# Weight blocks placed between the steps of a chunked linear attention, in a two-block transformer layer on one core

## The chip, the core and the metric

The kernel runs on one NeuronCore of one Trainium2 chip. The metric is the device time of one execution in microseconds (us), lower is better. The engines named are TensorE (PE, with its weight loads PEld), VectorE (DVE), ScalarE (ACT), GpSimd (POOL) and SyncE (SP, which issues the weight transfers).

## The reference, cut to what matters

The program computes two blocks on a sequence of 256 tokens of width 2048. The change touches only the token mixer of the second block:

```
def token_mixer(h, w_in, ...):
    z = h @ w_in                                  # 2048 columns in, 12304 out
    z_sg, q, k, v, og, g_lr, m_a, m_b = split(z)  # q, k: 1024 columns; v, og, m_a, m_b: 2048
    ...                                           # y_a from z_sg
    log_a = max(log_sigmoid(g_lr @ w_gate2 + b) / 16, -1)
    o = gla_chunked(q, k, v, log_a)               # 4 heads, 4 chunks of 64 tokens
    y_b = rmsnorm(o, gla_norm_g) * silu(og)
    merged = sigmoid(m_a) * (y_a @ w_proj_a) + sigmoid(m_b) * (y_b @ w_proj_b)
    return merged @ w_out

def gla_chunked(q, k, v, log_a):                  # for each head, over chunks of 64 tokens
    bcum = cumsum(log_a); b_last = bcum[last]
    q_in = q * dk**-0.5 * exp(bcum); k_in = k * exp(-bcum); k_st = k * exp(b_last - bcum)
    attn = causal(q_in @ k_in.T); o_intra = attn @ v
    step: o_inter = q_in @ state; state = state * exp(b_last) + k_st.T @ v
    return o_intra + o_inter
```

The output gate `og` is not needed by `gla_chunked`, and `m_b` is needed by neither the attention nor its normalisation.

## The kernel before, in words

Activations are kept transposed in SBUF as two fp32r tensors, a high part and the low rest (`HT`/`r_a` for the mixer's input, `YT`/`r_b` for the branch that is projected). A weight matrix is read in **blocks** of 512 output columns, and a block in **chunks** of 256 input rows (512 KB each). For each chunk SP issues a transfer into a ring of 5 slots (`raw_ring`), ACT rounds it to a high part (`act_hi`, L573, into one of 3 slots of `w_hi`), DVE subtracts that to leave the low part (`dve_lo`, L579, written over the raw slot), and PE multiplies (`pe_block_part`, L602): 2 tiles of 128 tokens x 2 row tiles x 3 products (high by high, high by low, low by high), 12 matmuls of 512 columns, into PSUM bank 0 for the first tile and bank 1 for the second. PE's last matmul of a chunk raises `pair_used`, for which the cast three chunks on and the transfer five chunks on wait. After the 8 chunks of a block ACT moves the two banks to SBUF and raises `acc_free`, for which the first matmuls of the next block wait.

All engines run programs written out by hand, in order, with semaphores. Nothing reorders them, so that an instruction whose semaphore is late holds up all that follow on its engine.

In the mixer the phase `qkvo` has 12 blocks: 0 and 1 are q, 2 and 3 are k, 4 to 7 are v, and 8 to 11 are `og`. All 12 are multiplied first, `og` with Silu at its evacuation. Then comes the linear attention, `gla_body(i)` for 4 heads. PE's steps in a head are: cumulative sums of the decay in banks 4 and 5 (L1050, L1051); transposes of the block sum (L1056, bank 6); transposes of `QIN` and `KIN` (L1063, banks 7 and 0); scores (L1069, bank 1); `delta(0)` (L1075, banks 2 and 3); scores by v (L1088, L1089), `inter(1)` (L1082) and `delta(1)`; `inter(2)` and `delta(2)`; `inter(3)`. Between two of these steps there is a hand-over: ACT copies, takes exponentials or evacuates (L1521 to L1540), DVE scales, masks and updates the state (L2116 to L2137), and PE waits. These matmuls are plain fp32, which the trace shows as two records each. After the heads, ACT and DVE normalise `o` (L1241, L2152), DVE multiplies by the gate (L2155), and PE transposes the product into `YT` (phase `yb`, L782, with ACT at L1215 and DVE at L1687 behind it). Then the phase `mb` starts: 4 blocks of 16 chunks, 8 of `m_b` from `HT`, evacuated through Sigmoid (L1452), and 8 of `w_proj_b` from `YT`, merged by DVE (L2088, L2089).

Of the kernel before, what the change touches and what calls it, by code (L numbers as in the profile page):

```python
# [19 lines left out]
P = 128  # L20
# [74 lines left out]
def build(nc, A, out, xs):  # L95
    ds = bass.ds
    ctx = ExitStack()
    with ctx:
# [296 lines left out]
        gl_qk, gl_dec, gl_decs, gl_tr, gl_qt = sem("gl_qk"), sem("gl_dec"), sem("gl_decs"), sem("gl_tr"), sem("gl_qt")  # L395
        gl_att, gl_dl, gl_st, gl_o, gl_of = (sem("gl_att"), sem("gl_delta"), sem("gl_state"),
# [375 lines left out]
        def _(pe):  # L772
# [268 lines left out]
            for i in range(12):  # L1041
                qkvo_body(i)
            pe.wait_ge(tr_free, TRN["gl"][0] + 4)
            pe.wait_ge(gl_a, 1)

            def gla_body(i):
                pe.wait_ge(gl_of, 2 * i + 1)
                for t in range(2):
                    la = LOGA[:, t, ds(i * GK, GK)]
                    nc.tensor.matmul(PS[:, 4 + t, 0:GK], CN[:, C_TRI:C_TRI + P], la, start=True, stop=True)  # L1050
                    nc.tensor.matmul(PS[:, 4 + t, GK:2 * GK], CN[:, C_BLK:C_BLK + P], la, start=True,  # L1051
                                     stop=True).then_inc(gl_cum, 1)
                pe.wait_ge(gl_bcs, 2 * i + 2)
# [25 lines left out]
                def inter(n):  # L1079
# [120 lines left out]
        def _(act):  # L1200
# [278 lines left out]
            si = evac_to("qkvo", ph, 7, 2, lambda t, b: ZQ[:, t, ds(b * NB, NB)], ACT.Silu)  # L1479
# [33 lines left out]
            for i in range(2, 9):  # L1513
                q_body(i, cp)
            for i in range(9, 12):
                q_body(i, si)
            si(11)

            def gla_body(i):
                act.wait_ge(gl_cum, 2 * i + 1)  # L1520
# [6 lines left out]
                nc.scalar.activation(E2, BCS[:, :, 0:GK], ACT.Exp, scale=-1.0).then_inc(gl_exp, 1)  # L1527
                act.wait_ge(gl_df, i + 1)
                nc.scalar.activation(E3, E3, ACT.Exp).then_inc(gl_exp, 1)
                act.wait_ge(gl_dec, i + 1)  # L1530
# [3 lines left out]
                for k, (dst, b) in enumerate(((QT, 7), (KT2, 0))):  # L1534
                    act.wait_ge(gl_tr, 2 * i + k + 1)
                    nc.scalar.copy(dst, PS[:, b, :].rearrange("p (d n) -> p d n", d=2)).then_inc(gl_qt, 1)
                for t in range(2):
                    act.wait_ge(gl_o, 2 * i + t + 1)
# [136 lines left out]
        def _(dve):  # L1675
# [433 lines left out]
            for i in range(3, 12):  # L2109
                for j in range(8):  # L2110
                    dve_lo(dve, PH["qkvo"], i, j)

            def gla_body(i):
                qs, ks = ZQ[:, :, ds(i * GK, GK)], ZQ[:, :, ds(GH * GK + i * GK, GK)]
                dve.wait_ge(gl_bcs, 2 * i + 2)
                TT(E3, BCS[:, :, GK:2 * GK], BCS[:, :, 0:GK], ALU.subtract).then_inc(gl_df, 1)  # L2116
                dve.wait_ge(gl_exp, 3 * i + 1)
                V.scalar_tensor_tensor(QIN, qs, GK ** -0.5, E1, ALU.mult, ALU.mult).then_inc(gl_qk, 1)
                dve.wait_ge(gl_exp, 3 * i + 2)
                TT(KIN, ks, E2, ALU.mult).then_inc(gl_qk, 1)  # L2120
                dve.wait_ge(gl_exp, 3 * i + 3)
                TT(KST, ks, E3, ALU.mult).then_inc(gl_qk, 1)
                for n in range(3):
                    dve.wait_ge(gl_dl, 3 * i + n + 1)
# [19 lines left out]
            V.tensor_scalar(SSO, SSO, 1.0 / GV, EPS, ALU.mult, ALU.add).then_inc(ms_ready, 1)  # L2144
            dve.wait_ge(rt_ready, m + 1)
# [11 lines left out]
            merge_loop("mb", 16, True)  # L2157
# [150 lines left out]
```

## Time and profile before

| | |
|---|---|
| median of 3 runs | 4530.18 us (4527.86 to 4532.74) |
| the profiled execution | 4539.61 us |
| its span in the profile | 4537.8 us |
| PE busy | 4114.8 us, 91% |
| DVE busy | 1732.0 us, 38% |
| ACT busy | 1631.0 us, 36% |
| granted TensorE clock, mean | 0.892 of 2.4 GHz |

The median is what the changed kernel is compared with, while durations come from the one profiled execution, which took 9.4 us (0.2%) more. "Busy" of PE counts modelled ends of matmuls: a PE that is busy may be running at half its clock, so the granted clock has to be read beside it. Times of rows are from the start of the span.

### The profile page before, as it was taken

What the parts mean: (1) busy time and instruction counts of PE and PEld (TensorE: products, weight loads), DVE (VectorE), ACT (ScalarE), POOL (GpSimd) and SP (SyncE); (2) the same over time, 40 slices, a digit from 0 to 9 for tenths busy, and PEclk for the clock granted to TensorE, in tenths of its full rate; (3) what the DMA queues carried; (4) which work ended last, traced back from release to release, by engine and by line L of the source; (5) the groups of instructions that cost most, each with busy time, mean ns of one, the idle gap of its engine ahead of it and who ended that gap; (6) DMA issues with size and microseconds to landing.
All of it is one profiled execution on the core that took longest, in us unless ns stands there. A gap on an engine that the chain in (4) does not pass through costs nothing.

```text
span 4537.8 us, 46263 instructions
## 1 busy us (share of the span) xinstructions
PE 4114.8 (91%) x19088; PEld 3106.5 (68%) x19088; DVE 1732.0 (38%) x2643; ACT 1631.0 (36%) x2550; POOL 69.1 (2%) x120
## 2 busy tenths in 40 slices
PE   5899979998899999989988989999789987999998
PEld 1466656676566667865666767787267767999886
DVE  0322233322223233333224545443255445666544
ACT  1222123334312123333344343444234455555433
POOL 3000000000001000000000000000000000000000
PEclk8899985569899999995598999999799998999999
DMA  9444420001245443320024555565045444666564
GB/s 316 141 147 141 148 77 1 1 18 35 75 148 167 158 139 95 115 82 1 6 65 121 191 149 163 171 188 169 0 155 171 158 138 127 195 193 193 181 199 153
DMA packets 350594, 577.49 MB, mean 127 GB/s; under 512 B 25252, under 2 KB 130868, under 8 KB 348208
## 3 DMA queue, kind: packets, MB, share of 16 engines
q1 hardware_dynamic: 344000, 549.39, 38.7%
q0 software_dynamic: 6384, 25.14, 1.8%
q8 instruction: 151, 2.47, 0.2%
q14 instruction: 59, 0.48, 0.0%
HBM read 570.26 MB, written 4.19 MB: 127 GB/s over the span
## 4 chain that ended last, share of the span: by engine, by line
PE 52%; DVE 5%; ACT 4%; issue 1%; DMA 0%; ACTq 0%; DVEq 0%
PE ps L602 32%; PE ps L1176 11%; PE ps L695 2%; PE ps L916 1%; DVE w_lo L579 1%; PE ps L686 1%; PE ps L885 1%; ACT w_hi L573 1%; PE ps L1075 1%; PE ps L1082 1%; PE ps L864 1%; ACT f_arena L1222 0%; PE ps L622 0%; DVE r_a L1689 0%; DVE r_b L1687 0%
## 5 line engine op out<-in xcount | busy, mean ns | idle before, releaser
L579 DVE TENSOR_TENSOR w_lo<-raw_ring,w_hi 128x1024 fp32r<-128x1024 f32 (+1 forms) x827 | 1003.1, 1223 | 1539.2 <-ACT w_hi L573 1530.9
L573 ACT CAST w_hi<-raw_ring 128x1024 fp32r<-128x1024 f32 (+1 forms) x827 | 858.6, 1049 | 1585.4 <-PE ps L602 751.0
L602 PE MATMUL ps<-w_hi,r_a 128*128 128x512 f32 x3552 | 1285.5, 403 | 74.8 <-DVE w_lo L579 49.4
L602 PE MATMUL ps<-w_lo,r_a 128*128 128x512 f32 x2624 | 1040.0, 396 | 0.0
L602 PEld LDWEIGHTS ps<-w_hi,r_a 128*128 128x128 f32 x3552 | 678.7, 191 | 346.0 <-issue 129.1
L602 PE MATMUL ps<-w_hi,r_b 128*128 128x512 f32 x2272 | 862.2, 399 | 9.3 <-DVE w_lo L579 4.2
L602 PEld LDWEIGHTS ps<-w_lo,r_a 128*128 128x128 f32 x2624 | 502.2, 191 | 105.3
L602 PEld LDWEIGHTS ps<-w_hi,r_b 128*128 128x128 f32 x2272 | 435.1, 192 | 114.3 <-DVE w_lo L579 11.4
L1176 PE MATMUL ps<-r_a,w_hi 128*128 128x256 f32 x2816 | 480.6, 277 | 3.0 <-DVE w_lo L579 3.0
L1176 PEld LDWEIGHTS ps<-r_a,w_hi 128*128 128x128 f32 x2816 | 425.5, 188 | 3.1 <-issue 3.1
L1176 PE MATMUL ps<-r_a,w_lo 128*128 128x256 f32 x1408 | 389.4, 277 | 0.0
L1176 PEld LDWEIGHTS ps<-r_a,w_lo 128*128 128x128 f32 x1408 | 265.2, 188 | 0.0
L695 PE MATMUL ps<-f_arena 128*128 128x64 f32 (+1 forms) x1072 | 226.8, 379 | 15.1 <-DVE f_arena L743 14.4
L637 PE MATMUL ps<-raw_ring,silu_c_t 128*2 128x512 f32 x768 | 201.0, 657 | 39.2 <-DMA raw_ring<-in_w_ada_dram 32.4
L695 PEld LDWEIGHTS ps<-f_arena 128*128 128x128 f32 x1072 | 220.8, 300 | 22.8 <-issue 22.0
L602 PE MATMUL ps<-w_hi,act_t 128*128 128x512 f32 x704 | 221.4, 395 | 5.8 <-DVE w_lo L579 5.4
L705 ACT ACTIVATE f_arena<-ps,neg_max 128x512 f32<-128x512 f32 (+1 forms) x164 | 99.9, 609 | 349.9 <-DVE neg_max L731 180.2
L686 PEld LDWEIGHTS ps<-consts,f_arena 128*128 128x128 f32 x536 | 84.8, 199 | 170.9 <-issue 106.7
L728 DVE TENSOR_REDUCE neg_max<-ps 128x1 f32<-128x512 f32 (+1 forms) x164 | 97.4, 594 | 187.4 <-PE ps L941 139.8
L916 PE MATMUL ps<-raw_ring,f_arena 128*128 128x192 f32 (+1 forms) x816 | 157.2, 355 | 8.0 <-ACT f_arena L1398 5.7
L686 PE MATMUL ps<-consts,f_arena 128*128 128x128 f32 x536 | 141.6, 402 | 20.7 <-ACT f_arena L714 14.5
L782 PE MATMUL ps<-consts,f_arena 128*128 128x128 f32 x508 | 91.3, 332 | 75.2 <-ACT f_arena L1236 35.6
(289 smaller groups left out, 3057.2 us busy)
## 6 DMA issues: line engine op xcount, KB each, us to landing
raw_ring<-in_w_in_dram SPq DMA_DIRECT2D x386, 512.0 KB, 3.7
raw_ring<-in_w_ada_dram SPq DMA_DIRECT2D x192, 512.0 KB, 3.9
raw_ring<-in_ffn_w_up_dram SPq DMA_DIRECT2D x176, 512.0 KB, 3.6
raw_ring<-in_w_out_dram SPq DMA_DIRECT2D x96, 512.0 KB, 3.7
raw_ring<-in_ffn_w_down_dram SPq DMA_DIRECT2D x88, 512.0 KB, 3.7
raw_ring<-in_w_proj_b_dram SPq DMA_DIRECT2D x32, 512.0 KB, 3.6
raw_ring<-in_w_proj_a_dram SPq DMA_DIRECT2D x16, 512.0 KB, 3.5
raw_ring<-in_w_qb_dram SPq DMA_DIRECT2D x24, 288.0 KB, 3.0
```

The lines of the kernel that those rows point to most:

```text
L573: nc.scalar.copy(WH[:, ph.s_slot(i, j), 0:n], RAW[:, ph.raw_slot(i, j), 0:n]).then_inc(hi_ready, 1)
L579: nc.vector.tensor_tensor(WL[:, ph.raw_slot(i, j), 0:n], RAW[:, ph.raw_slot(i, j), 0:n], WH[:, ph.s_slot(i, j), 0:n].bitcast(F32), ALU.sub ...
L602: mm = nc.tensor.matmul(PS[:, ti, 0:cols], X(x, k, t), W[w][:, kk * cols:(kk + 1) * cols], start=(k == 0 and q == 0), stop=(c == len(js) - ...
L637: mm = nc.tensor.matmul(PS[g:g + 2, 7, :], SCT[:, k, :], RAW[:, ph.raw_slot(i, j), kk * NB:(kk + 1) * NB], start=(k < ADAG), stop=(k >= KT ...
L686: tr = nc.tensor.transpose(PS[:, 6, q * P:q * P + P], PB[:, u % 2, q * P:q * P + P], ident)
L695: mm = nc.tensor.matmul(PS[:, 7, 0:vdim], PT[:, u % 2, q * P:q * P + P], V(u, kt), start=(q == 0), stop=(q == len(kts) - 1))
L705: ins = nc.scalar.activation(PB[:, k % 2, 0:w], PS[:, 4 + k % 2, 0:w], ACT.Exp, bias=NM[:, k % 2:k % 2 + 1], accum_out=SUM[:, k % 2:k % 2 ...
L728: mx = nc.vector.tensor_reduce(NM[:, k % 2:k % 2 + 1], PS[:, 4 + k % 2, 0:w], AX_X, ALU.max, negate=True)
L782: return [lambda b, t=t: nc.tensor.transpose(PS[:, b, t * P:t * P + P], src(t), ident) for t in range(T)]
L864: yield nc.tensor.matmul(PS[:, 4 + k % 2, 0:kr.stop - kr.start], QTA[r, t * P:t * P + P], KTA[r, kr], start=True, stop=True)
L916: mm = nc.tensor.matmul(PS[:, t, o:o + cols], X[:, k, t * P:t * P + P], RAW[:, ph.raw_slot(i, j), kk * cols:(kk + 1) * cols], start=(k == ...
L1176: mm = nc.tensor.matmul(PS[:, 4 * b + f, 0:256], W[w][:, kk * 256 + f % 2 * P:kk * 256 + f % 2 * P + P], HT[:, x, k, :], start=(k == 0 and ...
```

## The change

Three things are done, all inside the mixer's second branch:

1. `qkvo` blocks 8 to 11 (`og`) are taken out of the row of 12 and multiplied inside the heads of the linear attention. Each head now holds one block, with one chunk ahead of each of the eight places at which PE waits for ACT or DVE. ACT and DVE have their `act_hi` and `dve_lo` for these chunks written between their own steps, two chunks ahead of PE. The blocks are evacuated plain, in the head.
2. Banks 0 and 1 now hold those blocks, so the transposed `KIN` goes to bank 6 and the scores to bank 7. PE's transposes of `KIN` get a new wait on `gl_decs`, since ACT has to have read bank 6.
3. The first 8 chunks of `mb` (block 0 of `m_b`) are multiplied straight after the last head, while ACT and DVE normalise. ACT now takes the Silu of `og` there in two instructions of 128 x 2048, and DVE multiplies by the gate in two halves (new semaphore `gl_og`). PE no longer waits for all 16 evacuated transposes before the first `w_proj_b` chunk, but for as many as each chunk reads.

The core of the diff, PE, ACT and DVE in this order. `si` is the evacuation of a block with Silu, `cp` the plain one. Left out are, on PE, four more `next(og)` ahead of the waits for `gl_qk` 3i+3, `gl_att`, `gl_st` 3i+2 and `gl_st` 3i+3, and on ACT and DVE eight `next` each in `gla_body`, and on ACT `cp(8 + i)` ahead of the wait for `inter(3)`:

```
-            for i in range(12):
+            for i in range(8):
                 qkvo_body(i)
+            def og_chunks():
+                for b in range(8, 12):
+                    for c in range(8):
+                        pe_block_part(pe, PH["qkvo"], b, S8, c, 2, NB, hT, range(2), AC["qkvo"][b])
+                        yield
+            og = og_chunks()
             def gla_body(i):
+                next(og)
                 pe.wait_ge(gl_of, 2 * i + 1)
...
+                next(og)
                 pe.wait_ge(gl_bcs, 2 * i + 2)
...
+                next(og)
                 pe.wait_ge(gl_qk, 3 * i + 2)
-                for X, b in ((QIN, 7), (KIN, 0)):
+                for X, b in ((QIN, 7), (KIN, 6)):
+                    if b == 6:
+                        pe.wait_ge(gl_decs, i + 1)
...
+                next(og)
                 pe.wait_ge(gl_qt, 2 * i + 2)
...
-                        mm = nc.tensor.matmul(PS[:, 1, t * P:t * P + P], KT2[:, d, t * P:t * P + P],
+                        mm = nc.tensor.matmul(PS[:, 7, t * P:t * P + P], KT2[:, d, t * P:t * P + P],
...
             for i in range(GH):
                 gla_body(i)
+            pe_block(pe, PH["mb"], 0, S8, 2, NB, hT, range(2), AC["mb"][0])
             pe.wait_ge(gl_of, 2 * GH + 2)
             for k in range(KT):
                 group(TRN["yb"][0] + k, tr_tiles(lambda t: ZQ[:, t, OGO + k * P:OGO + k * P + P], 2))
-            pe.wait_ge(tr_free, TRN["yb"][0] + KT)
...
+                for c in range(8):
+                    if i == 0:
+                        pe.wait_ge(tr_free, TRN["yb"][0] + 2 * c + 2)
+                    pe_block_part(pe, PH["mb"], i, list(range(8, 16)), c, 2, NB, yT, range(2), acc_at("mb", i, 2, 1))
```
```
-            for i in range(9, 12):
-                q_body(i, si)
-            si(11)
+            act_hi(act, ph, 8, 0)
+            cp(7)
+            act_hi(act, ph, 8, 1)
+            def og_his():
+                seq = [(ph, b, j) for b in range(8, 12) for j in range(8)] + [(PH["mb"], 0, 0), (PH["mb"], 0, 1)]
+                for p, b, j in seq[2:]:
+                    act_hi(act, p, b, j)
+                    yield
...
             nc.scalar.copy(JG[0][:, 0:8], SSO.rearrange("p t h -> p (t h)")).then_inc(ss_ready, 1)
+            act_hi(act, PH["mb"], 0, 2)
             root("gla", SSO, RIO)
+            act_hi(act, PH["mb"], 0, 3)
+            ogs = ZQ[:, :, OGO:OGO + D]
+            nc.scalar.activation(ogs[:, 0], ogs[:, 0], ACT.Silu)
+            act_hi(act, PH["mb"], 0, 4)
+            nc.scalar.activation(ogs[:, 1], ogs[:, 1], ACT.Silu).then_inc(gl_og, 1)
+            for j in range(5, 9):
+                act_hi(act, PH["mb"], 0, j)
+            sig_evac("mb", 0)
             to_hi("yb", KT, lambda k: YT[:, 0, k, :], 256)
-            sig_loop("mb", 16)
+            sig_loop("mb", 16, 1)
```
```
             V.tensor_scalar(SSO, SSO, 1.0 / GV, EPS, ALU.mult, ALU.add).then_inc(ms_ready, 1)
+            dve_lo(dve, PH["mb"], 0, 2)
...
                     ins = V.scalar_tensor_tensor(o, o, RIO[:, t, h:h + 1], GNB, ALU.mult, ALU.mult)
+                    if h % 2:
+                        dve_lo(dve, PH["mb"], 0, 3 + 2 * t + h // 2)
             L(ins)
-            TT(og, og, ZQ[:, :, VO:VO + D], ALU.mult).then_inc(gl_of, 1)
+            dve.wait_ge(gl_og, 1)
+            TT(og[:, 0], og[:, 0], ZQ[:, 0, VO:VO + D], ALU.mult)
+            dve_lo(dve, PH["mb"], 0, 7)
+            TT(og[:, 1], og[:, 1], ZQ[:, 1, VO:VO + D], ALU.mult).then_inc(gl_of, 1)
+            dve_lo(dve, PH["mb"], 0, 8)
```

The order on PE, in the first half of a head, before (L1051 is the second of the cumulative sums, L1056 and L1063 transposes, L1069 the scores, L1075 `delta`):

```order
L1051 MATMUL ps<-gla_arena,consts 128x256
L1056 MATMUL ps<-consts,gla_arena 128x128 x4
L1063 MATMUL ps<-consts,f_arena 128x128 x8
L1069 MATMUL ps<-gla_arena 128x128 x4
L1075 MATMUL ps<-gla_arena,f_arena 128x512 x2
```

The same place now (the lines have moved: L1066 was L1056, L1076 was L1063, L1083 was L1069, and L603, which was L602, is the matmul of a weight block):

```order
L1066 MATMUL ps<-consts,gla_arena 128x128 x4
L603 MATMUL ps<-w_hi,r_a 128x512
...
L603 MATMUL ps<-w_hi,r_a 128x512
L1076 MATMUL ps<-consts,f_arena 128x128 x8
L603 MATMUL ps<-w_hi,r_a 128x512
...
L603 MATMUL ps<-w_hi,r_a 128x512
L1083 MATMUL ps<-gla_arena 128x128 x4
```

Each group of L603 rows holds 12 matmuls, one chunk. Nothing is taken out of the head itself.

The order on ACT in a head now (L574 is the cast `act_hi`, L1547 the copy of v, L1550 the copies of the sums, L1552, L1553 and L1556 the exponentials, L1559 the decay, L1565 the copies of the transposed q and k, L1574 and L1575 the evacuation of `o`, L1279 the evacuation of the weight block):

```order
L1550 COPY gla_arena<-ps 128x512 x2
L1552 ACTIVATE f_arena<-gla_arena 128x512
L1553 ACTIVATE f_arena<-gla_arena 128x512
L574 CAST w_hi<-raw_ring 128x1024
L1556 ACTIVATE f_arena<-f_arena 128x512
L574 CAST w_hi<-raw_ring 128x1024
L1559 ACTIVATE decay<-ps 128x8
L574 CAST w_hi<-raw_ring 128x1024
L1565 COPY gla_arena<-ps 128x512 x2
L574 CAST w_hi<-raw_ring 128x1024 x2
L1574 ACTIVATE f_arena,gla_sums<-ps 128x512
```

Before, none of the four L574 rows stood there. The casts now stand ahead of steps that PE and DVE wait for.

The order on DVE in the normalisation after the heads, before (L2146 is the reciprocal of the root, L2152 the scaling, L2155 the product with the gate):

```order
L2146 RECIPROCAL gla_rinv<-gla_rinv 128x8
L2152 SCALAR_TENSOR_TENSOR f_arena<-f_arena,gla_rinv,gla_arena 128x512 x8
L2155 TENSOR_TENSOR f_arena<-f_arena 128x2x2048
L1687 TENSOR_TENSOR r_b<-ps,r_b 128x256 x16
```

And now (L580 is `dve_lo`, L2208, L2214, and L2220 with L2222 are the three steps):

```order
L2208 RECIPROCAL gla_rinv<-gla_rinv 128x8
L2214 SCALAR_TENSOR_TENSOR f_arena<-f_arena,gla_rinv,gla_arena 128x512 x2
L580 TENSOR_TENSOR w_lo<-raw_ring,w_hi 128x1024
...
L2214 SCALAR_TENSOR_TENSOR f_arena<-f_arena,gla_rinv,gla_arena 128x512 x2
L580 TENSOR_TENSOR w_lo<-raw_ring,w_hi 128x1024
L2220 TENSOR_TENSOR f_arena<-f_arena 128x2048
L580 TENSOR_TENSOR w_lo<-raw_ring,w_hi 128x1024
L2222 TENSOR_TENSOR f_arena<-f_arena 128x2048
```

Five L580 rows now stand between the reciprocal and the last product, and one more ahead of the reciprocal.

## Rows read from the trace of the kernel before

**Rows 1.** The page: busy time of the engines.
```profile
PE 4114.8 (91%) x19088; PEld 3106.5 (68%) x19088; DVE 1732.0 (38%) x2643; ACT 1631.0 (36%) x2550; POOL 69.1 (2%) x120
```

**Rows 2.** Stretches: length, busy time of the engines, clock, DMA share, GB/s.
```profile
3104.80:3127.20 22.40, 22.27 (x97) 17.95 (x97) 9.69 (x9) 9.39 (x10) 0.00 (x0) 1.00 0.65 188
3161.00:3298.00 137.00, 99.98 (x226) 41.40 (x224) 28.05 (x44) 29.72 (x59) 0.00 (x0) 0.75 0.02 6
```

**Rows 3.** PE's groups in 3161 to 3298: busy, mean ns, idle before.
```profile
L1082 PE MATMUL ps<-gla_arena 128*64 128x512 f32 x48 | 29.2, 740 | 12.0 <-DVE gla_arena L2133 12.0
...
L1088 PE MATMUL ps<-gla_arena 128*128 128x512 f32 x8 | 8.3, 1141 | 6.9 <-DVE gla_arena L2137 6.9
...
L1063 PE MATMUL ps<-consts,f_arena 128*128 128x128 f32 x32 | 7.1, 394 | 6.6 <-DVE f_arena L2120 6.6
...
L1050 PE MATMUL ps<-gla_arena,consts 128*128 128x256 f32 x16 | 5.1, 398 | 3.8 <-ACT f_arena L1540 3.8
```

**Rows 4.** PE in the first head, in order of time: start, duration.
```profile
3172.18 3.78 PE L1075 MATMUL ps<-gla_arena,f_arena 64*128 64x512 f32 x4
...
3187.45 1.93 PE L1082 MATMUL ps<-gla_arena 128*64 128x512 f32 x4 [1.50 <-DVE gla_arena L2133]
...
3189.31 1.98 PE L1075 MATMUL ps<-gla_arena,f_arena 64*128 64x512 f32 x4
...
3192.79 3.40 PE L1082 MATMUL ps<-gla_arena 128*64 128x512 f32 x4 [1.50 <-DVE gla_arena L2133]
```

**Rows 5.** Stretches of 4 us around the end of the first head; columns as rows 2.
```profile
3186.00:3190.00 4.00, 2.55 (x6) 0.92 (x7) 1.39 (x2) 0.00 (x0) 0.00 (x0) 1.00 0.00 0
3190.00:3194.00 4.00, 2.50 (x6) 0.64 (x5) 1.41 (x2) 0.00 (x0) 0.00 (x0) 0.89 0.00 0
...
3198.00:3202.00 4.00, 2.09 (x11) 1.35 (x9) 1.34 (x3) 3.36 (x6) 0.00 (x0) 1.00 0.00 0
```

**Rows 6.** ACT and DVE in order of time: a chunk's cast and subtraction, then a head's hand-overs.
```profile
3144.85 1.05 ACT L573 CAST w_hi<-raw_ring 128x1024 fp32r<-128x1024 f32 x1 [2.12 <-PE ps L602]
3145.93 1.23 DVE L579 TENSOR_TENSOR w_lo<-raw_ring,w_hi 128x1024 fp32r<-128x1024 f32 x1 [1.94 <-ACT w_hi L573]
...
3162.19 1.04 ACT L1521 COPY gla_arena<-f_arena 128x1024 f32<-128x1024 f32 x1 [0.32 <-PE ps L1051]
3163.14 1.07 ACT L1524 COPY gla_arena<-ps 128x512 f32<-128x512 f32 x2
3164.23 1.28 ACT L1526 ACT_TABLE_LOAD   x1
...
3165.52 0.63 ACT L1526 ACTIVATE f_arena<-gla_arena 128x512 f32<-128x512 f32 x1
...
3166.18 0.69 DVE L2118 SCALAR_TENSOR_TENSOR f_arena<-f_arena 128x512 f32<-128x512 f32 x1 [1.25 <-ACT f_arena L1526]
```

**Rows 7.** The chain of waits after the last head: start, length, what.
```profile
3299.47 1.28 ACT L1241
3300.76 0.22 ACT gla_rinv L1241
...
3301.24 5.40 DVE f_arena L2152 x8
...
3306.66 4.43 DVE f_arena L2155
...
3318.66 1.84 issue
3320.50 24.90 PE ps L602 x96
...
3368.02 12.18 PE ps L602 x52
```

**Rows 8.** ACT in order of time: an activation of 128 x 2048.
```profile
2918.74 1.92 ACT L1493 ACTIVATE f_arena<-gla_arena 128x2048 f32<-128x2048 f32 x1
```

**Rows 9.** A stretch of later transposes (L782); columns as rows 2.
```profile
3516.00:3518.00 2.00, 2.00 (x12) 1.00 (x10) 2.00 (x7) 2.00 (x6) 0.00 (x0) 1.00 0.00 0
```

More of the change, by code:

```diff
@@ L1084, in inter @@
                     return mm
+                next(og)
                 pe.wait_ge(gl_qk, 3 * i + 3)
                 delta(0)
+                next(og)
                 pe.wait_ge(gl_att, i + 1)
@@ L1092, in gla_body @@
                 delta(1)
+                next(og)
                 pe.wait_ge(gl_st, 3 * i + 2)
@@ L1095, in gla_body @@
                 delta(2)
+                next(og)
                 pe.wait_ge(gl_st, 3 * i + 3)
@@ L1512, in _ @@
                            (3, log_abs, ()), (4, log_exp, ()), (5, log_ln, ())])
-            for i in range(2, 9):
+            for i in range(2, 8):
                 q_body(i, cp)
-            for i in range(9, 12):
-                q_body(i, si)
-            si(11)
+            act_hi(act, ph, 8, 0)
[6 more added lines that the diff above has]
+                    yield
+            og = og_his()
             def gla_body(i):
+                next(og)
                 act.wait_ge(gl_cum, 2 * i + 1)
@@ L1527, in gla_body @@
                 nc.scalar.activation(E2, BCS[:, :, 0:GK], ACT.Exp, scale=-1.0).then_inc(gl_exp, 1)
+                next(og)
                 act.wait_ge(gl_df, i + 1)
                 nc.scalar.activation(E3, E3, ACT.Exp).then_inc(gl_exp, 1)
+                next(og)
                 act.wait_ge(gl_dec, i + 1)
@@ L1533, in gla_body @@
                                      ACT.Exp).then_inc(gl_decs, 1)
-                for k, (dst, b) in enumerate(((QT, 7), (KT2, 0))):
+                next(og)
+                for k, (dst, b) in enumerate(((QT, 7), (KT2, 6))):
                     act.wait_ge(gl_tr, 2 * i + k + 1)
                     nc.scalar.copy(dst, PS[:, b, :].rearrange("p (d n) -> p d n", d=2)).then_inc(gl_qt, 1)
+                next(og)
+                next(og)
                 for t in range(2):
+                    if t:
+                        next(og)
+                        next(og)
+                        cp(8 + i)
                     act.wait_ge(gl_o, 2 * i + t + 1)
@@ L2108, in _, with og_los @@
                         V.tensor_scalar(G[:, 0:2048], LM, 1.0 / 16.0, -1.0, ALU.mult, ALU.max).then_inc(gl_a, 1)
-            for i in range(3, 12):
+            for i in range(3, 8):
                 for j in range(8):
                     dve_lo(dve, PH["qkvo"], i, j)
+            dve_lo(dve, PH["qkvo"], 8, 0)
+            dve_lo(dve, PH["qkvo"], 8, 1)
+            def og_los():
+                seq = [(PH["qkvo"], b, j) for b in range(8, 12) for j in range(8)] + [(PH["mb"], 0, 0), (PH["mb"], 0, 1)]
+                for p, b, j in seq[2:]:
+                    dve_lo(dve, p, b, j)
+                    yield
+            og = og_los()
             def gla_body(i):
+                next(og)
                 qs, ks = ZQ[:, :, ds(i * GK, GK)], ZQ[:, :, ds(GH * GK + i * GK, GK)]
@@ L2116, in gla_body @@
                 TT(E3, BCS[:, :, GK:2 * GK], BCS[:, :, 0:GK], ALU.subtract).then_inc(gl_df, 1)
+                next(og)
                 dve.wait_ge(gl_exp, 3 * i + 1)
@@ L2120, in gla_body @@
                 TT(KIN, ks, E2, ALU.mult).then_inc(gl_qk, 1)
+                next(og)
                 dve.wait_ge(gl_exp, 3 * i + 3)
                 TT(KST, ks, E3, ALU.mult).then_inc(gl_qk, 1)
+                next(og)
+                next(og)
                 for n in range(3):
+                    if n:
+                        next(og)
                     dve.wait_ge(gl_dl, 3 * i + n + 1)
@@ L2137, in gla_body @@
                         V.copy_predicated(ATT, bc(CN[:, C_TRI:C_TRI + P].bitcast(I32), 2),
-                                          PS[:, 1, 0:256].rearrange("p (t n) -> p t n", t=2)).then_inc(gl_att, 1)
+                                          PS[:, 7, 0:256].rearrange("p (t n) -> p t n", t=2)).then_inc(gl_att, 1)
+                next(og)
             for i in range(GH):
```

10 lines of the change are left out of this document (4 added, 6 removed).

## The prediction, made before the changed kernel was run

> **What bounds the kernel now.** I read the page's busy times first. PE is busy 91% of the span and no other engine over 38% [rows 1], so that time is won where PE idles or runs at half clock. Then two stretches side by side [rows 2]: a block of the `qkvo` phase, where PE is busy 22.27 of 22.40 us at a granted clock of 1.00, and the four heads, 137.00 us with PE busy 99.98 at 0.75. That stretch begins when block 11 ends (3161) and holds no weight block at all; DVE and ACT are busy 28 and 30 us in it, and the DMA share is 0.02. So PE idles 37.0 us there, and of the 100 in which it works a part is at 1.2 GHz. PE's groups name most of it [rows 3]: 12.0 + 6.9 + 6.6 + 3.8 = 29.3, each time for the ACT or DVE step just before; by difference 7.7 are left for L1056 and L1069. Third, the chain of waits after the last head [rows 7]: the last `inter(3)` ends at 3298.0, the first `mb` matmul starts at 3320.5, that block takes 24.9, and its `w_proj_b` part ends at 3368.0. That is 70.0 us for 16 chunks, against 44 at the rate of rows 2.
>
> **Part 1, the heads.** Before: four `og` blocks at 22.4 [rows 2] are 89.6, and with the heads' 137.0 it is 226.6 us.
>
> After, PE has the same matmuls and, if nothing is late, no gaps. A block is 96 matmuls; inside a block they start 0.2288 us apart (22.27 / 97 is 0.2296 with its boundary), so a chunk of 12 takes 2.75 and a block 22.0. The boundary gap of about 0.4 goes, since the evacuation now has other PE work beside it. A head's own matmuls are taken at full clock. L1075 is the yardstick: the same four records take 3.78 us early in the head and 1.98 later, L1082's four 1.93 [rows 4]. One group starts 1.87 after the other. There are seven such groups (three `delta`, three `inter`, one for scores by v); without the modelled end of the last record, which overlaps what follows, 1.75 each, 12.3. L1050 has 16 records of 256 columns, and L1051 as many: half of the columns of those above, so about 0.22 a record, and with 8 in a head 1.7. L1063 is 7.1 us in four heads for 32 records, mostly at half clock, so at full clock about 1.1 a head with the part that is already fast; L1069 has as many records of the same shape, and L1056 half as many: 1.1 and 0.5 [rows 3]. The sum is 16.7, and I take 17.
>
> So PE needs 39.0 a head. Now whether hand-overs are hidden. Each has a chunk of 2.75 ahead of it. Durations on ACT and DVE [rows 6]: a cast 1.05, a subtraction 1.23, a copy of v 1.04, the two copies of sums 1.07, an exponential about 0.6, a product about 0.65. I follow the tightest one, q and k, from the end of the first cumulative sum (time 0). ACT: v to 1.1, sums to 2.1, two exponentials to 3.3, cast to 4.35 (its wait is for the chunk before the sums, long used). DVE: subtraction to 5.6, QIN to 6.3, KIN to 6.95. PE: second sum to 0.9, chunk to 3.6, L1056 to 4.1, chunk to 6.8. PE is ready 0.15 before KIN. All others have slack: the copies that L1069 waits for end at 9.1 where PE comes at 10.7; state and mask after `delta(0)` take 1.7 of the next chunk's 2.75, and the later state updates 1.4; the last evacuation of `o` takes 1.25 of the next head's first chunk. The new wait on `gl_decs` ends at 6.2, before PE comes. The casts for chunks two ahead are each released by a chunk that PE has already done, because the order is the same on all three engines. What is queued behind each of them is the hand-over, and that is in the sum above. I add 0.2 a head, and once 1.3 in the first head for the table load of the exponential, which sits in this tightest chain [rows 6]. ACT needs about 17 us a head and DVE as much (a quarter of rows 2's 29.7 and 28.1, plus 8 casts or subtractions), under half of PE's 39.
>
> After: 4 x (39.0 + 0.2) + 1.3 = 158.1. Gain: 226.6 - 158.1 = 68.5 us, of which 37 is idle time, about 30 the clock, less 1.5 for waits, and the rest boundaries and tails.
>
> **The clock.** This is the term that has to be argued. In 3186 to 3194 PE was busy 5 of 8 us, with half-filled arrays only (64 rows or 64 columns), and the clock was 1.00 for the first four and fell within the next (0.89). `inter(3)` then ran slow, 3.40 us of L1082 without a gap [rows 4], and from 3198, just after it, the clock was 1.00 again [rows 5]. So PE's continuous work in the heads' own shapes brings the clock up, and after the change over half of the time is dense blocks. I take 1.00 for the whole stage.
> The Trainium skill, in TensorE: Matmul & The Clock Gate, section "A second HAM failure mode: psum-queue depth-cycling", says that a kernel which cycles through PSUM banks can idle in such small pieces between groups that the clock swings all the same, and the changed stage visits seven banks. By it the present mean of 0.75 would stay, which is priced below as a rival; the dense stretch in rows 2, which alternates two banks, does not swing.
>
> **Part 2, normalisation and first `mb` block.** Time 0 is the end of `inter(3)` (3298.0 before). PE: eight chunks from 0 to 22.0 if their low parts are there. ACT: evacuation to 1.25, sums copied 1.5, cast 2 to 2.5, table and root to 4.0, cast 3 to 5.05, table 1.28 and Silu 1.92 [rows 7, 8] to 8.25, cast 4 to 9.3, second Silu to 11.2, cast 5 to 12.25, then casts at PE's pace. DVE: subtraction 2 to 3.75, reciprocal 4.2, scaling 1.35 a pair (5.40 / 4) with subtractions 3, 4, 5, 6 between, which end at 6.8, 10.55, 13.5 and 16.1. PE wants them at 8.2, 11.0, 13.7 and 16.5: just in time. Half of the gate product is 2.2 (4.43 / 2): first to 18.3, subtraction 7 to 19.55 (PE wants it at 19.2: 0.35 late), second to 21.8, so `gl_of` is there when PE ends the block at 22.3. The whole chain of 13.1 us from 3298.0 to the transposes has grown by the subtractions, but lies beside PE's block. Then 16 transposes at DVE's pace: Sigmoid evacuates to 23.4, DVE starts at 23.85 and takes 0.42 for each, PE may issue the last four earlier and goes on at about 29.2. Before, 1.84 lay between the last split and the first matmul; that goes. Eight chunks are 22.0, plus 0.7 because chunk 9's cast stands behind all evacuations: 51.9. The clock: it was 1.00 at later transposes at this pace [rows 9]; I allow 1.1 us. So 53.0 in place of 70.0, a gain of 17.
> Bounds: 19 if nothing of this is late, and 10 if the chain, six subtractions and two Silus come one after another (13.1 + 7.4 + 3.8, which is 2.3 past the block) and the clock falls as in rows 7 (24.9 for 22.0).
> The Trainium skill, in ScalarE: Activation LUTs, section "What ACT_TABLE_LOAD costs", has every change of table drain for 1.38 us more behind the 1.28 of the load. Two such changes stand ahead of cast 4; by the rule subtraction 4 ends at 13.3, PE loses 2.3 us, and the sum is 4446. The trace has the root start 0.01 us after the load [rows 7], so I leave it at nothing.
>
> **Sum.** 68.5 + 17 = 85.5 from the profiled 4539.6 gives 4454.1; the median of the runs is 9.4 below the profiled execution, so from 4530.2 it gives 4444.7, and I say 4444. After this stage nothing is moved. The extra transfers are none; they only move into a stretch whose DMA share is 0.02.
>
> **Rivals.**
> A. The clock keeps swinging. For: mean 0.75 in the same stage today, and the half-filled arrays remain. Against: rows 5. If only the heads' own matmuls stay as slow as now, they take their 100 us, not 68: 4444 + 32 = 4476. If all 156 us run at a mean of 0.75, it is 208: 4496.
> B. Hand-overs are late. For: the tightest one has no slack, and both queues are strict. Each of eight places late by half a cast (0.5) costs 4 x 8 x 0.5 = 16, by a whole one 34: 4460 to 4478. Against: seven of eight have over 1 us in hand by the rows.
> C. The change doesn't shorten the stage, because each chunk is only put in front of a hand-over and nothing lies beside it: then the four blocks cost 88 in the heads as outside, and only part 2 is gained: 4513. Against: the casts are two chunks ahead in all three programs.
> D. Slower: PE falls to 1.2 GHz for the interleaved stage, dense chunks too, since small gaps at every hand-over keep it there. Of 156 us of PE work the share g run at half clock adds 156 g; above g = 0.55 it eats the 85.5. At g = 1 it is 4600. Against: the clock rose within the heads even with the gaps [rows 5].
>
> **Chances.** Forecast (4434 to 4456) 0.72; B 0.13; A 0.09; C 0.03; D 0.03. The low end is the forecast with 17 a head at 15.5, 6 less, and 19 in part 2, with 2 for the runs: 4434. The high end takes in B's smaller case and most of its larger: 4472. A measurement of this kernel tells about 0.2% (9 us) from no change. Faster by more than that: 0.95, within it 0.02, slower 0.03.
>
> **What would show it.** Right: from the first `og` chunk to the last `inter(3)` some 158 us at a clock near 1.00, L1075's four records about 1.9 us in every place, PE idle under 6 us in it, and 52 to 54 us from there to the second `mb` block. Step by step wrong: idle at the transposes of q and k means B; a clock under 0.9 in the heads means A or D; PE waiting for `w_lo` in the first `mb` block means that part 2's chain is longer than worked out.

## The result, and the profile after

| | before | changed |
|---|---|---|
| median | 4529.32 us (4527.86 to 4532.74, 4 runs) | 4449.82 us (4448.65 to 4451.54, 4 runs) |
| ratio, with its 95% interval | | 0.9824 (0.9807 to 0.9841) |
| profiled execution, and its span | 4539.61, 4537.8 | 4451.54, 4449.8 |
| mean granted clock | 0.892 | 0.903 |

The kernel became 79.5 us (1.8%) faster. 4444 was forecast, with 4434 to 4472 as the range. The runs before are those of the table ahead of the prediction and a fourth of 4528.46 us. One of the five executions of `e7_yb_between` below took 9150.53 us and is left out of its median.

The page's busy times. PE works less than before [rows 1], because more of its work runs at full clock:

```profile
PE 4076.3 (92%) x19088; PEld 3089.6 (69%) x19088; DVE 1728.8 (39%) x2644; ACT 1634.3 (37%) x2552; POOL 69.1 (2%) x120
```

Three stretches of the changed kernel, with the columns of rows 2: the heads with the four `og` blocks; the first `mb` block beside the normalisation; and from there to the second `mb` block:

```profile
3066.70:3227.80 161.10, 159.95 (x611) 101.64 (x609) 66.26 (x77) 66.67 (x100) 0.00 (x0) 1.00 0.36 106
3227.83:3250.00 22.17, 22.17 (x99) 18.17 (x99) 18.39 (x19) 16.59 (x18) 0.00 (x0) 1.00 0.58 182
3250.00:3280.38 30.38, 27.54 (x129) 20.85 (x127) 16.75 (x28) 15.18 (x27) 3.35 (x6) 1.00 0.70 250
```

Two things are to be seen: the clock, 1.00 in all three, where the heads had 0.75 [rows 2]; and PE busy 159.95 of 161.10 us. ACT and DVE are busy 66 us each, 41% of the stretch.

The chain of waits through the second head (start, length, what; L1059 is a cumulative sum, L1066 and L1076 the transposes, L1083 the scores, L1089 `delta`, L1104 and L1105 scores by v, L1096 `inter`, and L603 x12 a chunk):

```profile
3110.92 0.43 PE ps L1059 x2
...
3112.65 2.76 PE ps L603 x12
3115.41 0.44 PE ps L1066 x4
3115.85 2.77 PE ps L603 x12
3118.62 0.96 PE ps L1076 x8
3119.58 2.76 PE ps L603 x12
3122.34 0.89 PE ps L1083 x8
3123.23 2.77 PE ps L603 x12
3126.00 1.91 PE ps L1089 x4
3127.91 2.96 PE ps L603 x12
...
3146.07 1.86 PE ps L1096 x4
3147.93 2.95 PE ps L603 x12
3150.88 0.43 PE ps L1059 x2
```

Nothing but PE stands in it: every hand-over of ACT and DVE is over before PE comes, the tightest (`KIN`, for L1076) by less than 0.1: DVE ends it at 3118.43, and PE's first transpose starts at 3118.49 by its own record. A head takes 3150.88 - 3110.92 = 39.96 us, block included; before it took 137.0 / 4 = 34.3 without one [rows 2]. L1089's four records take 1.91 us in every place (before, L1075's took 3.78 or 1.98 [rows 4]).

The chain from the last `inter(3)` on, answering to rows 7:

```profile
3227.83 22.20 PE ps L603 x96
...
3251.42 4.16 PE ps L783 x24
3255.58 2.77 PE ps L603 x12
...
3258.36 10.82 DMA raw_ring<-in_w_proj_b_dram
...
3271.66 7.13 PE ps L603 x30
...
3280.38 22.26 PE ps L603 x96
```

The 22.5 us from the last `inter(3)` to the first `mb` matmul [rows 7] are gone. The whole stretch of 16 chunks takes 3280.38 - 3227.83 = 52.55 us, where it took 70.0. What is new is one transfer of a `w_proj_b` chunk that took 10.82 us, with PE waiting 2.1 us behind it.

Where the spans' 88.0 us went: 4.7 lie ahead of the first `og` chunk, which PE reaches at 3071.7 us before and 3066.9 after (the first cumulative sum at 3069.7 less one chunk of 2.76). The code up to there is the same, and in the eleven traces of this case the place lies between 3064.9 and 3081.4, so these 4.7 us are no part of the change. The heads with their blocks give 226.4 - 160.9 = 65.5, the stretch behind them 17.4, and what follows 0.4. So the change is worth 82.9 us by the two profiles and 79.5 by the medians.

### The profile page after: what moved, and what is told of

Same layout as the page of the kernel before. It is cut to its first block, busy times and chain, and to the rows that moved or that the text cites. A ratio compares the mean times of both kernels' runs of the same rounds, so it can differ in the third digit from the quotient of the medians.

```text
span 4449.8 us, 46273 instructions
## 1 busy us (share of the span) xinstructions
PE 4076.3 (92%) x19088; PEld 3089.6 (69%) x19088; DVE 1728.8 (39%) x2644; ACT 1634.3 (37%) x2552; POOL 69.1 (2%) x120
## 4 chain that ended last, share of the span: by engine, by line
PE 53%; DVE 4%; ACT 3%; issue 1%; DMA 0%; ACTq 0%; DVEq 0%
PE ps L603 32%; PE ps L1195 11%; PE ps L696 2%; PE ps L917 1%; DVE w_lo L580 1%; PE ps L687 1%; PE ps L886 1%; ACT w_hi L574 1%; PE ps L865 1%; PE ps L1089 1%; PE ps L1096 1%; ACT f_arena L1241 0%; PE ps L783 0%; PE ps L623 0%; DVE r_a L1733 0%
## 5 line engine op out<-in xcount | busy, mean ns | idle before, releaser
L580 DVE TENSOR_TENSOR w_lo<-raw_ring,w_hi 128x1024 fp32r<-128x1024 f32 (+1 forms) x827 | 1003.6, 1223 | 1511.3 <-ACT w_hi L574 1505.8
L574 ACT CAST w_hi<-raw_ring 128x1024 fp32r<-128x1024 f32 (+1 forms) x827 | 860.9, 1051 | 1573.2 <-PE ps L603 730.0
L603 PE MATMUL ps<-w_hi,r_a 128*128 128x512 f32 x3552 | 1287.9, 402 | 73.3 <-DVE w_lo L580 51.0
L603 PE MATMUL ps<-w_lo,r_a 128*128 128x512 f32 x2624 | 1040.2, 396 | 0.0
L603 PEld LDWEIGHTS ps<-w_hi,r_a 128*128 128x128 f32 x3552 | 676.8, 191 | 353.8 <-issue 137.6
L603 PE MATMUL ps<-w_hi,r_b 128*128 128x512 f32 x2272 | 865.0, 400 | 11.5 <-DVE w_lo L580 6.3
L603 PEld LDWEIGHTS ps<-w_lo,r_a 128*128 128x128 f32 x2624 | 501.5, 191 | 104.9
L603 PEld LDWEIGHTS ps<-w_hi,r_b 128*128 128x128 f32 x2272 | 436.0, 192 | 115.0 <-DVE w_lo L580 10.8
L696 PE MATMUL ps<-f_arena 128*128 128x64 f32 (+1 forms) x1072 | 227.6, 380 | 15.1 <-DVE f_arena L744 14.4
L603 PE MATMUL ps<-w_hi,act_t 128*128 128x512 f32 x704 | 220.5, 394 | 5.8 <-DVE w_lo L580 5.4
L687 PE MATMUL ps<-consts,f_arena 128*128 128x128 f32 x536 | 142.0, 403 | 20.4 <-ACT f_arena L715 13.8
L603 PEld LDWEIGHTS ps<-w_hi,act_t 128*128 128x128 f32 x704 | 132.9, 189 | 36.1 <-issue 5.6
```

What stands on the lines that cost most here:

```text
L574: nc.scalar.copy(WH[:, ph.s_slot(i, j), 0:n], RAW[:, ph.raw_slot(i, j), 0:n]).then_inc(hi_ready, 1)
L580: nc.vector.tensor_tensor(WL[:, ph.raw_slot(i, j), 0:n], RAW[:, ph.raw_slot(i, j), 0:n], WH[:, ph.s_slot(i, j), 0:n].bitcast(F32), ALU.sub ...
L603: mm = nc.tensor.matmul(PS[:, ti, 0:cols], X(x, k, t), W[w][:, kk * cols:(kk + 1) * cols], start=(k == 0 and q == 0), stop=(c == len(js) - ...
L687: tr = nc.tensor.transpose(PS[:, 6, q * P:q * P + P], PB[:, u % 2, q * P:q * P + P], ident)
L696: mm = nc.tensor.matmul(PS[:, 7, 0:vdim], PT[:, u % 2, q * P:q * P + P], V(u, kt), start=(q == 0), stop=(q == len(kts) - 1))
```

## The experiments

### Each part alone

`e1_heads_only` undoes the third part of the change. ACT and DVE have their casts and subtractions of that block behind the transposes again, as they were:

```
-            pe_block(pe, PH["mb"], 0, S8, 2, NB, hT, range(2), AC["mb"][0])
             pe.wait_ge(gl_of, 2 * GH + 2)
...
+            pe.wait_ge(tr_free, TRN["yb"][0] + KT)
```

> The og blocks stay inside the heads; the first mb block is again multiplied after the transposes, as before the change. My accounting from the two traces gives the heads 65.6 us and the normalisation 17.4 us of the gain: then this is 4464 to 4467 us, and heads plus first blocks take 161 us at a clock of 1.00. If the chunks had only been put in front of the hand-overs with nothing beside them (rival C), the heads would be worth nothing and this would be at 4529.

Measured: 4466.74 us beside 4531.36 for the kernel before, ratio 0.9854 (0.9822 to 0.9885).

`e2_norm_only` undoes the first part, on ACT and DVE likewise, and keeps the plain evacuation of `og` and the new banks:

```
-            for i in range(8):
+            for i in range(12):
                 qkvo_body(i)
...
             def gla_body(i):
-                next(og)
                 pe.wait_ge(gl_of, 2 * i + 1)
```

> The og blocks go back in front of the heads (evacuated plainly, Silu in the normalisation as in the changed kernel), and only the first mb block lies beside the normalisation. By the same accounting 17 us: 4512. If the two parts shared a gain (for instance the clock at the start of mb, which would be high anyway once the heads keep PE busy), this one would be worth more, up to 22 us (4507), and e1 less.

Measured: 4516.11 us beside 4531.36, ratio 0.9960 (0.9941 to 0.9979). The two gains, 64.6 and 15.3 us, add up to 79.9, against the change's own 79.5. The intervals are 14 and 9 us wide to either side, so that a sum as close as this is partly luck. From the two traces, `e1_heads_only` first (L1096 and L603 as above), each from the last `inter(3)` to the second `mb` block:

```profile
3225.77 1.88 PE ps L1096 x4
...
3251.01 9.49 DMA raw_ring<-in_w_in_dram
...
3294.04 16.05 PE ps L603 x69
```
```profile
3293.82 22.21 PE ps L603 x96
...
3324.37 12.22 DMA raw_ring<-in_w_proj_b_dram
...
3339.06 8.72 PE ps L603 x30
...
3349.38 22.26 PE ps L603 x96
```

In `e1` the heads with their blocks take 160.9 us, as in the changed kernel, and the stretch behind them takes 3294.04 - 3227.65 = 66.4 us, where it took 70.0: part 1 alone wins 3.6 us there. Half of that is the gap of 1.84 us ahead of the first weight matmul [rows 7], 0.04 in `e1`, because the first two casts and subtractions of `mb` now stand in the last head. In `e2` the heads keep their 137.2 us, and the stretch takes 55.6 us in place of 70.0, 14.4 less. By the rows the parts so add up (3.6 + 14.4 = 18.0 behind the heads, against 17.4 for both), but they aren't divided as I had them: part 1 is worth about 69 us and part 2 about 14, not 65.5 and 17.4.

### What the interleaving itself does

`e3_bunched` has the same eight chunks in each head, all at its start, on ACT and DVE too:

```
             def gla_body(i):
-                next(og)
+                for _q in range(8):
+                    next(og)
                 pe.wait_ge(gl_of, 2 * i + 1)
...
-                next(og)
                 pe.wait_ge(gl_bcs, 2 * i + 2)
```

> As the changed kernel, but each head's eight chunks stand in one row at its start on PE, ACT and DVE, so that all blocks are in the same place but no hand-over has a chunk ahead of it. If the gain of the heads is what lies beside the hand-overs together with the clock, it is all lost: 4450 + 65 = 4515, PE idle about 37 us in the stage and a clock of 0.5 to 1.0 within the heads. If the clock alone (22 us of dense work in every 56) were kept up by the blocks next to each head, the L1089 and L1096 groups would stay fast and it would be near 4485.

Measured: 4516.99 us beside 4531.36, ratio 0.9960 (0.9941 to 0.9979), the first of the two outcomes. The first row is a window that nearly is the stage (which runs from 3069.1, the end of the blocks of v, to 3292.1, the end of the last `inter(3)`: 223.0 us). Below it are pieces of the first and second head (L1087 is `delta`, L1094 `inter`):

```profile
3066.70:3290.00 223.30, 187.69 (x617) 115.08 (x616) 68.36 (x77) 68.28 (x101) 0.00 (x0) 0.85 0.28 80
```
```profile
3102.53 3.72 PE ps L1087 x4
...
3122.72 3.59 PE ps L1094 x4
3126.31 22.20 PE ps L603 x96
...
3158.74 3.72 PE ps L1087 x4
```

The 22.2 us of dense work in front of a head don't keep the clock up in it: in both heads the first `delta` is at half speed, 10 us after the block. PE idles 223.3 - 187.7 = 35.6 us, and the granted clock of the stage is 0.85, as it is in the kernel before over the same stage (3071.7 to 3298.0). So the same chunks in another order leave 3.3 of the heads' 65.5 us (226.4 - 223.0). The whole gain of 14.4 us against the kernel before is what `e2_norm_only` has without them (15.3), within the noise.

### The clock alone

`e4_warm` is the kernel before with the changed kernel's banks and dummy matmuls at PE's waits, and no block moved:

```
+            def warm(n=5):
+                for _w in range(n):
+                    nc.tensor.matmul(PS[:, 0, :], HT[:, 0, 0, 0:P], RA[:, 0:NB], start=True, stop=True)
             def gla_body(i):
+                warm()
                 pe.wait_ge(gl_of, 2 * i + 1)
...
+                warm(10)
                 pe.wait_ge(gl_qk, 3 * i + 2)
```

> The kernel before, with the changed kernel's banks (and its wait on gl_decs), and dummy matmuls at PE's waits in the heads: 5, 5, 10, 2, 0, 6, 6 and 6 matmuls of 128x512 fp32r into the unused bank 0, 0.23 us each at full clock, some 9.2 us a head against 9.3 us of idle. No block is moved, so what is gained is the clock alone. If the clock is worth what I worked out, a head falls from 34.5 to some 26.5 us and the kernel to 4497. If the granted clock follows something else than how busy PE is, the heads keep 34.5 us and it stays at 4529 or becomes slower.

Measured: 4510.62 us beside 4531.36, ratio 0.9956 (0.9939 to 0.9973). The heads in one row, and a part of the third head (L1050 is the dummies, L1094 `inter`, L1087 `delta`):

```profile
3171.70:3287.00 115.30, 111.86 (x384) 59.28 (x384) 28.06 (x44) 29.84 (x61) 0.00 (x0) 1.00 0.02 5
```
```profile
3246.71 1.91 PE ps L1087 x4
3248.62 1.59 PE ps L1050 x6
3250.21 1.86 PE ps L1094 x4
3252.07 1.91 PE ps L1087 x4
3253.98 1.59 PE ps L1050 x6
```

Matmuls that compute nothing made the kernel 20.7 us faster: the clock is 1.00 and the heads end after 114.2 us (3171.7 to 3285.9) instead of 137.0. That is 5.7 us a head where I expected 8, since a group of six takes 1.59 us where the wait was 1.5, and the groups for the long waits don't fit either. So the clock is shown as a cause by itself: nothing that the program needs was done sooner for want of work, and at least 22.8 us of the heads' gain is the clock.

### The long transfer

`e5_pool_spread` spreads the large loads of POOL over later blocks:

```
             pool.wait_ge(tr_free, TRN["yb"][0] + KT)
+            pool.wait_ge(acc_free, AC["mb"][2][0] + 2)
+            pool.dma_start(MEM[:, 0], mem_src[:, 0]).then_inc(mem_in, 16)
+            pool.wait_ge(acc_free, AC["mb"][3][0] + 2)
+            pool.dma_start(MEM[:, 1], mem_src[:, 1]).then_inc(mem_in, 16)
+            pool.wait_ge(acc_free, AC["mb"][4][0] + 2)
             pool.dma_start(PN, ...).then_inc(pn_in, 16)
-            pool.dma_start(MEM, ...).then_inc(mem_in, 16)
```

> The changed kernel, with the three large loads that POOL issues at the end of the transposes (PN 1 MB, MEM 2 MB) spread over mb blocks 1 and 2. In the changed kernel one w_proj_b transfer took 10.8 us beside them and PE waited 2.1 us for it. If that is contention, the wait and the long transfer go: 2 us less, 4448, and the stretch from the last inter(3) to the second mb block falls from 52.6 to 50.5 us. If the transfer is long for a reason of its own (the strided w_proj_b, the queue's order), the stretch stays at 52.6.

Measured: 4445.30 us beside 4533.10, ratio 0.9809 (0.9788 to 0.9830). The stretch by windows, and its chain (L608 is the chunk's matmul):

```profile
3229.45:3279.69 50.24, 49.48 (x225) 39.11 (x225) 35.12 (x46) 31.75 (x45) 0.00 (x0) 1.00 0.53 166
```
```profile
3257.21 20.89 PE ps L608 x90
```

The eight chunks run through with no transfer in the chain, and the stretch is 50.24 us, 2.3 less than 52.55. The long transfer was contention with POOL's 3 MB. The medians can't tell this from the changed kernel (the ratios' intervals overlap).

The price isn't the same in every trace. PE waited 2.1 and 2.4 us in the two traces of the changed kernel, and 3.1, 3.5 and 3.9 us in those of `e3_bunched`, `e2_norm_only` and `e6_full_array`, whose loads are where the changed kernel has them. In these three the granted clock was 0.50 to 0.57 in the 4 us behind the wait, and the 30 matmuls there took 8.7 to 9.4 us in place of 7.13.

### Half and full array

`e6_full_array` lets `delta` read all 128 rows and `inter` write all 128 partitions, so its state and output are other sums than the reference's:

```
                 def delta(n):
-                    r = slice(64 * (n % 2), 64 * (n % 2) + 64)
+                    r = slice(0, P)
...
-                        mm = nc.tensor.matmul(PS[r, 4 + n // 2, :], QT[:, d, n * 64:n * 64 + 64], STATE[:, d, :],
+                        mm = nc.tensor.matmul(PS[:, 4 + n // 2, :], QT[:, d, n // 2 * P:n // 2 * P + P], STATE[:, d, :],
```

> The changed kernel, with delta reading all 128 rows and inter writing all 128 partitions in place of 64 (the sums of state and output are then other ones; everything else is the same instruction for instruction). In the changed kernel the four records of delta take 1.91 us and of inter 1.86, against 1.72 for scores by v in the same form, and a chunk behind one of them 2.96 us against 2.76 elsewhere. If this is the price of switching between half and full array, the groups fall to about 1.72 and the chunks to 2.76: 1.7 us a head, 7 in all, 4443. If it comes from their being released by DVE or from the state's operand, nothing changes.

Measured: 4445.94 us beside 4533.10, ratio 0.9821 (0.9796 to 0.9847). From the chain of its third head (L1090 is `delta`, L1097 `inter`, L1059 the cumulative sum that begins a head):

```profile
3147.05 0.43 PE ps L1059 x2
...
3162.12 1.72 PE ps L1090 x4
3163.84 2.76 PE ps L603 x12
...
3180.71 1.72 PE ps L1097 x4
3182.42 2.77 PE ps L603 x12
3185.19 0.43 PE ps L1059 x2
```

Every group is 1.72 and every chunk 2.76 us, and a head 38.14 in place of 39.96: the switch between half and full array was the price, 7.3 us in all. That it is the switch, and not the half array as such, agrees with the changed kernel's records: of `delta`'s, the longest takes 693 ns and the median 589, so that a group loses its time once. The times couldn't have told this: the ratio is the changed kernel's 0.9824 within its interval. In the profiled execution the wait for the long transfer was 3.9 us, and from the last `inter(3)` to the end of PE's last `w_proj_b` tile before the merge it took 54.9 us, against 3278.79 - 3227.83 = 51.0 in the changed kernel.

### Transposes with chunks between them

`e7_yb_between` adds to `e5_pool_spread` (the loop with all 16 transposes goes, and ACT and DVE have three casts and subtractions between their evacuations):

```
                 for c in range(8):
                     if i == 0:
+                        for k in range(4 * c, min(4 * c + 4, KT)):
+                            group(TRN["yb"][0] + k, tr_tiles(...))
                         pe.wait_ge(tr_free, TRN["yb"][0] + 2 * c + 2)
```

> On top of e5_pool_spread: the 16 transposes of the normalised product come in four groups of four, with one w_proj_b chunk behind each on PE, and casts and subtractions between the evacuations on ACT and DVE. In the changed kernel PE spends 5.5 us in these transposes at the pace of DVE (0.42 us each) for 1.8 us of its own work. Worked out: 4 x (0.45 + 2.75) = 12.8 us for the transposes and four chunks in place of 5.5 + 11.0, so 3.7 less than e5, and 48.8... 46.8 us from the last inter(3) to the second mb block; 4444. If DVE (1.7 + 1.23 us for each four) is late, 1 to 2 us of it are lost.

Measured: 4446.9 us beside 4533.10, ratio 0.9810 (0.9788 to 0.9831). The expectation of 3.7 us failed: against `e5` (0.9809) nothing is gained in time. Its stretch by windows and its chain:

```profile
3228.89:3278.40 49.51, 48.24 (x225) 39.20 (x225) 35.30 (x46) 30.91 (x45) 0.00 (x0) 1.00 0.55 168
```
```profile
3252.02 0.77 DVE r_b L2237 x2
...
3252.83 3.04 PE ps L608 x12
3255.87 0.87 PE ps L788 x8
```

The stretch of 49.51 us is only 0.7 less than `e5`'s. I had given four transposes of two tiles 0.45 us, and they take 0.87 (eight records of 0.11), so that all 16 are 3.5 us of work and not 1.8. Of the 5.5 us only 2.0 was waiting, and the first chunk still waits 0.9 for DVE.

### All of it together

`e8_whole` adds to `e7_yb_between` the whole-array form of `e6`, with zeros where the other half would come in:

```
+        KST3 = F[:, T0 + 3072:T0 + 3840].rearrange("p (s n) -> p s n", s=3)
+        QTM = G[:, 5376:6144].rearrange("p (s d n) -> p s d n", s=3, d=2)
...
+                        mm = nc.tensor.matmul(PS[:, 2 + d, :], KST3[:, n, d * P:d * P + P], VST[:, n // 2, :],
...
+                        mm = nc.tensor.matmul(PS[:, 4 + n // 2, :], QTM[:, n - 1, d, :], STATE[:, d, :],
...
+                for n in (1, 2, 3):
+                    ins = nc.scalar.copy(QTM[:, n - 1, :, 64 * (n % 2):64 * (n % 2) + 64], QT[:, :, 64 * n:64 * n + 64])
+                ins.then_inc(gl_qm, 1)
...
+                TT(KST3[0:64, 0, :], ks[0:64, 0, :], E3[0:64, 0, :], ALU.mult)
+                TT(KST3[64:128, 1, :], ks[64:128, 0, :], E3[64:128, 0, :], ALU.mult)
+                TT(KST3[0:64, 2, :], ks[0:64, 1, :], E3[0:64, 1, :], ALU.mult).then_inc(gl_qk, 1)
```

> e7_yb_between with delta and inter over the whole array and the right sums: the state's keys are kept in three slots whose other 64 rows are zero, and the scaled q in three slots whose other 64 columns are zero, so the added rows and columns add zeros. DVE has three products of 64 rows in place of one of 128 in each head, and ACT three small copies more, both off the tight chain of q and k. e6_full_array showed 38.15 us a head against 39.95; if the same holds here, the stretch from the first og chunk to the last inter(3) falls by 7.2 us, and the kernel is 7 us under e7 and some 10 us under the changed kernel in the same call. If the extra ACT copies or DVE products delay a hand-over, part of the 7.2 comes back as PE idle in front of L1109 or L1094's place.

Beside it ran the changed kernel, without an edit.

> The changed kernel itself once more, beside e8_whole on the same chip and against the same runs of the kernel before, so that e8 is compared in one call: about 4450, heads 39.95 us each, 52.6 us from the last inter(3) to the second mb block, of which about 2 us are the wait for one w_proj_b transfer.

Measured: `e8_whole` 4441.03 us, ratio 0.9797 (0.9773 to 0.9821) to the kernel before (4532.90); the changed kernel 4451.13, ratio 0.9813 (0.9793 to 0.9834). A head of `e8_whole` by windows, and the chain where the next one begins and where `mb` does (L1066 is the cumulative sum, L1103 `inter`, L610 a chunk's matmul):

```profile
3184.77:3222.90 38.13, 38.13 (x154) 26.88 (x153) 16.77 (x23) 17.38 (x30) 0.00 (x0) 1.00 0.39 110
```
```profile
3146.63 0.43 PE ps L1066 x2
...
3184.77 0.43 PE ps L1066 x2
...
3218.43 1.72 PE ps L1103 x4
3220.15 22.02 PE ps L610 x96
...
3269.47 22.26 PE ps L610 x96
```

A head takes 38.14 us with PE never idle in it, so the extra copies and products are covered, and the stretch behind the heads takes 49.3. By the rows that is 7.3 + 3.2 = 10.5 us under the changed kernel, and 10.1 by the medians. The two ratios' intervals overlap, so the difference from the changed kernel is shown by the profile rather than by the times. Against the kernel before, the times show the gain.

## Why the prediction was right

**The heads.** Forecast 158.1 us, measured 160.9; forecast gain 68.5, measured 65.5. Its parts by the rows: PE's idle time fell from 37.0 to 1.1 us, all of it in the first head ahead of the transposes of q and k, where I had put 1.3 for the table load and 0.2 for each head. In the other three the tightest hand-over was just in time, less than 0.1 us early, where 0.15 late was worked out. The heads' own matmuls went from 100.0 to 68.5 us (160.9 - 1.1 - 91.3 for the chunks). Most of these 31.5 us is the clock, of which `e4_warm` shows at least 22.8 with no block moved; the rest includes the modelled ends of groups that nothing followed, and isn't separated. They come to 17.1 us a head, where I took 17, and that is partly luck: the six groups of `delta` and `inter` take 1.86 to 1.91 and not 1.75, 0.8 more in all, while transposes and scores take 2.3 and not 2.7, and 0.3 was rounding. The mis-sized term is the chunk: 32 x 2.75 = 88 was taken, and 15 of the 32 take 2.96, 91.3 in all, for the switch of array form behind `delta` and `inter`. With 0.5 more for the heads' own matmuls and 1.0 less for the waits, that is the 2.8 us between forecast and result.

**The clock.** Taken as 1.00 from the return of the clock just after `inter(3)` [rows 5], and it is 1.00. `e3_bunched` shows that blocks next to the heads don't do this (L1087 at 3.72 us again), and `e4_warm` that work at the waits does, whatever it computes. The changed stage visits all eight banks (not seven, as the prediction has it) at 1.00, with PE idle 1.1 of 160.9 us. The Trainium skill (TensorE: Matmul & The Clock Gate, section "A second HAM failure mode: psum-queue depth-cycling") has the clock swing from small idle times between the groups of a kernel that cycles through banks. These idle times are what the change took away, so that visiting the banks alone doesn't bring the swing here, and the rest of the rule isn't tested.

**Part 2.** Forecast 53.0 us, measured 52.55, and that it is so close is luck. The first `w_proj_b` chunk was forecast 29.2 us after the last `inter(3)` and stands in the chain at 27.75, since DVE began its 16 subtractions earlier (23.1, not 23.85) and started them 0.34 us apart, not 0.42. From there I had 22.0, 0.7 for a late cast, which didn't show, and 1.1 for the clock, which stayed at 1.00: 23.8. It took 24.8, because the transfer, for which I had put nothing, cost 2.1. The prediction said that the extra transfers are none; it overlooked POOL's 3 MB. Before the change they fell on a PE at a granted clock of 0.50 and 0.78 (in the first two pieces of 4 us from 3320.5), which did 25 matmuls there and waited for none. In `e1_heads_only` they fall on the same block at a clock of 1.00: PE does 36 in the first 8 us and then waits 0.9 us. The two Silus and the subtractions were in time, as said: the block of 96 matmuls has no wait (22.20 us). The drain of 1.38 us that the Trainium skill (ScalarE: Activation LUTs, section "What ACT_TABLE_LOAD costs") gives for each change of table would have held up chunk 4 by 2.3 us, by the prediction's estimate. No such wait shows: the root and the first Silu start 0.02 and 0.01 us after the 1.28 us of their loads, and subtraction 4 ends 10.3 us after the last `inter(3)`.

**The sum.** 85.5 was forecast, and the profiles have 82.9 in the stage. The remaining 3.4 us to the medians' 79.5 are not located: the profiled execution of the kernel before lay 10.3 us over its median and that of the changed kernel 1.7 over its own. Of the 8.6 us between, 4.7 are ahead of the stage and 0.4 behind it, and where the rest lies is open.

**The rivals.** A (the clock swings) and D (slower, at half clock) are ruled out by the clock of 1.00; B (late hand-overs) and C (nothing lies beside the chunks) by PE's idle time of 1.1 us and a chain with PE alone in it from the second head on. `e3_bunched` shows what C would have cost: 4517, where 4513 was given.

## What to carry to other kernels

Where PE waits for ACT or DVE in a chain of short steps, independent matmuls between the steps are worth the idle time and nearly as much again for the clock, if they stand ahead of each wait; the same work in one row next to the chain was worth 3.3 us of the 65.5 here. Work out each hand-over against the filler in front of it, on each in-order queue, casts for later fillers included: one filler of 2.75 us covered all but one step here. After such a change look at what a slow stage used to hide, such as large loads that now meet a PE at full rate.

## What the runs showed of the hardware

- At each change between matmuls on 64 rows, matmuls into 64 columns and matmuls over the whole array, PE lost 0.14 to 0.20 us: four records of `delta` took 1.91 us and of `inter` 1.86 against 1.72 over the whole array, and the chunk behind them 2.96 against 2.76. Padding with zeros to the whole array took all of it away (`e6_full_array`, `e8_whole`).
- Dummy matmuls of 9.2 us a head made the heads 5.7 us a head faster (`e4_warm`). 22 us of dense work right in front of a head did not keep it fast: 10 us after it `delta` ran at half speed (`e3_bunched`).
- A transfer of 512 KB, where the median of its kind is 3.6 us, stood in the chain for 10.8 us beside 3 MB from POOL (11.2 to 12.6 in four other traces), and 2.3 us of the stretch went when these were spread (`e5_pool_spread`).
